# Two FFNs of a two-block transformer kernel: conditioning sums one unit later, conditioning additions in units 1 to 3 of a step

## What is computed

```python
cond = jax.nn.silu(c)
for i in range(DEPTH):                                   # DEPTH = 2
    mod = (cond @ ada_w[i] + ada_b[i]).reshape(b_, 3, 3, D_MODEL)
    h = adaln(x, norm_g[i, 0], mod[:, 0, 0], mod[:, 0, 1])
    x = x + 0.5 * (1.0 + mod[:, 0, 2][:, None, :]) * swiglu(h, ffn_w_in[i, 0], ffn_w_out[i, 0])
    ...                                                  # a mixer, then a second swiglu sublayer
def swiglu(h, w_in, w_out):                              # w_in (1024, 5632), w_out (2816, 1024)
    g, u = jnp.split(h @ w_in, 2, axis=-1)
    return (jax.nn.silu(g) * u) @ w_out
```

## Time and profile before

| what | value |
|---|---|
| median of three runs | 4431.83 us (4430.81 to 4432.5) |
| span of the profiled execution, first to last instruction | 4428.0 us |
| TensorE matmul busy | 3972.1 us, 90% |
| VectorE busy | 1926.5 us, 44% |
| ScalarE busy | 1401.3 us, 32% |
| chain of work that ended last: TensorE, VectorE, ScalarE | 78%, 9%, 6% |

### The profile page before, as it was taken

The page is one execution under the profiler, slowest core; times in us unless marked ns, Lnnn a source line. Parts: engine busy times, 40 slices in busy tenths (PEclk is TensorE's granted clock), DMA queues, the critical chain, the costliest instruction groups (busy, mean ns, idle before and its releaser), DMA issues.

```text
span 4428.0 us, 45107 instructions
## 1 busy us (share of the span) xinstructions
PE 3972.1 (90%) x16532; PEld 3063.7 (69%) x16532; DVE 1926.5 (44%) x2693; ACT 1401.3 (32%) x2072; POOL 145.5 (3%) x106
## 2 busy tenths in 40 slices
PE   6999599999999789999777789999987786998999
PEld 5887488878877347887344668778862465787887
DVE  6632775333332533333345554443335447444332
ACT  3222322232233533323333332332233333323221
POOL 1000200000000000000000000000001000000000
PEclk8999799999999689999887779999997885999999
DMA  7733376333333002333110113323330110232332
GB/s 258 240 113 88 106 254 208 93 89 95 94 89 89 0 1 79 97 95 113 29 34 5 43 38 96 91 86 96 95 97 5 34 44 5 76 99 78 99 93 88
DMA packets 626887, 390.79 MB, mean 88 GB/s; under 512 B 17088, under 2 KB 584256, under 8 KB 625600
## 3 DMA queue, kind: packets, MB, share of 16 engines
q1 hardware_dynamic: 621376, 376.82, 29.0%
q10 hardware_dynamic: 5376, 12.14, 0.8%
HBM read 386.81 MB, written 2.10 MB: 88 GB/s over the span
## 4 chain that ended last, share of the span: by engine, by line
PE 78%; DVE 9%; ACT 6%; issue 3%; DMA 2%; POOL 1%; SPq 0%; ACTq 0%; DVEq 0%; POOLq 0%
PE bank L1611 21%; PE bank L1613 21%; PE bank L1612 21%; PE bank L1770 3%; DMA work<-in_ada_w 1%; PE bank L1738 1%; ACT w_hi L638 1%; PE bank L1762 1%; PE bank L1718 1%; PE bank L1626 1%; DVE ada_acc L1039 1%; PE bank L1627 1%; PE bank L1628 1%; PE bank L1857 1%; PE bank L1637 1%
## 5 line engine op out<-in xcount | busy, mean ns | idle before, releaser
L1022 DVE TENSOR_TENSOR w_lo<-stage,w_hi 128x1024 fp32r<-128x1024 f32 x587 | 720.3, 1227 | 1825.5 <-ACT w_hi L638 1825.4
L1611 PE MATMUL bank<-h_hi,w_hi 128*128 128x512 f32 x3128 | 1229.2, 393 | 46.7 <-DVE h_lo L1274 32.3
L1613 PE MATMUL bank<-h_hi,w_lo 128*128 128x512 f32 x3128 | 1223.2, 391 | 0.0
L1612 PE MATMUL bank<-h_lo,w_hi 128*128 128x512 f32 x3128 | 1222.4, 391 | 0.0
L638 ACT ACTIVATE w_hi<-stage 128x1024 fp32r<-128x1024 f32 x587 | 622.0, 1060 | 1852.2 <-PE bank L1613 1761.8
L1611 PEld LDWEIGHTS bank<-h_hi,w_hi 128*128 128x128 f32 x3128 | 591.1, 189 | 178.0 <-DVE h_lo L1274 34.6
L1612 PEld LDWEIGHTS bank<-h_lo,w_hi 128*128 128x128 f32 x3128 | 591.3, 189 | 123.2 <-issue 1.4
L1613 PEld LDWEIGHTS bank<-h_hi,w_lo 128*128 128x128 f32 x3128 | 590.3, 189 | 124.3
L1613 PE MATMUL bank<-a_hi,w_lo 128*128 128x512 f32 x1056 | 410.8, 389 | 0.0
L1611 PE MATMUL bank<-a_hi,w_hi 128*128 128x512 f32 x1056 | 410.8, 389 | 0.0
L1612 PE MATMUL bank<-a_lo,w_hi 128*128 128x512 f32 x1056 | 410.8, 389 | 0.0
(11 more groups left out here) (243 smaller groups left out, 3664.6 us busy)
## 6 DMA issues: line engine op xcount, KB each, us to landing
stage<-in_ffn_w_in SPq DMA_DIRECT2D x176, 512.0 KB, 3.9
stage<-in_w_in SPq DMA_DIRECT2D x108, 512.0 KB, 3.9
stage<-in_w_gate_up SPq DMA_DIRECT2D x88, 512.0 KB, 3.8
ada_stage<-in_ada_w SPq DMA_DIRECT2D x128, 256.0 KB, 4.4
work<-in_ada_w SPq DMA_DIRECT2D x128, 256.0 KB, 6.0
stage<-in_ffn_w_out SPq DMA_DIRECT2D x64, 512.0 KB, 4.1
stage<-in_w_down SPq DMA_DIRECT2D x32, 512.0 KB, 3.9
stage<-in_ffn_w_out SPq DMA_DIRECT2D x32, 384.0 KB, 3.4
```

Of the source, the lines that this page charges most:

```text
L1022: nc.vector.tensor_tensor(w_lo[:, w * WORDS:(w + 1) * WORDS], stage[:, slot * WORDS:(slot + 1) * WORDS], w_hi[:, w * WORDS:(w + 1) * WORDS ...
L1611: nc.tensor.matmul(dst, wh, chunk(hi, k), start=first and a == 0, stop=False)
L1612: nc.tensor.matmul(dst, wh, chunk(lo, k), start=False, stop=False)
L1613: ins = nc.tensor.matmul(dst, wl, chunk(hi, k), start=False, stop=last and a == len(ks) - 1)
```

## The change

Two things change, in the first two FFNs alone.

1. The table of VectorE's additions goes from 6, 6, 4, 0 at the places c = 0, 1, 2, 3 of a step to 0, 6, 5, 5.
2. The sum of vector j on TensorE, which stood at the end of step j behind unit 4j + 3, stands in step j + 1 between its units 0 and 1. VectorE's `ada_finish` goes from the end of step j to place c = 1 of step j + 1, between the split and `prod`. One step more is written out for this behind the loop.

```diff
-ADA_ADDS = [0, 6, 12, 16, 16]
+ADA_ADDS = [0, 0, 6, 11, 16]
...
-                def step_in(j, ada):
+                def step_in(j, ada, finish):
                     for c in range(4):
...
                         convert(c + 2, j)
+                        if c == 1 and finish:
+                            ada_finish(j, 1)
                         if c % 2:
...
-                    if ada:
-                        ada_finish(j)
...
-                    looped(dve, count, lambda j: step_in(j, True))
-                    with dve.Fori(count, FC // 2) as j:
-                        step_in(j, False)
+                    step_in(0, True, False)
+                    with dve.Fori(1, count) as j:
+                        step_in(j, True, True)
+                    step_in(count, False, True)
+                    with dve.Fori(count + 1, FC // 2) as j:
+                        step_in(j, False, False)
...
-                def step_in(j, ada):
+                def step_in(j, add):
                     for c in range(4):
                         p = n.pair + c // 2
+                        if c == 1 and add:
+                            ada_sum(j, 1)
...
-                    if ada:
-                        ada_sum(j)
...
```

More of the change, by code:

```diff
@@ L1040, in ada_add, with ada_finish @@
                         .then_inc(ada_added, 1)
-            def ada_finish(v=0):
-                dve.wait_ge(mod_summed, n.vec - ADA_FIRST + v + 2)
-                col = (n.vec + v) * DC
+            def ada_finish(v, back):
+                dve.wait_ge(mod_summed, v + (n.vec - ADA_FIRST - back + 2))
+                col = v * DC + (n.vec - back) * DC
                 dst = mod[:, col:col + DC] if isinstance(v, int) else mod[:, bass.ds(col, DC)]
@@ L1119, in step_in @@
                                                     ALU.subtract).then_inc(a_ready, 1)
-                    if ada:
-                        ada_finish(j)
                 count = ADA_IN.get(i, 0)
                 if count:
-                    looped(dve, count, lambda j: step_in(j, True))
-                    with dve.Fori(count, FC // 2) as j:
-                        step_in(j, False)
+                    step_in(0, True, False)
[4 more added lines that the diff above has]
+                        step_in(j, False, False)
                 else:
-                    looped(dve, FC // 2, lambda j: step_in(j, False))
+                    looped(dve, FC // 2, lambda j: step_in(j, False, False))
                 n.vec += count
@@ L1630, in first_pair, with ada_sum @@
                             ins.then_inc(unit_done, 1)
-            def ada_sum(v=0):
-                pe.wait_ge(ada_added, (n.vec - ADA_FIRST + v + 1) * ADA_PER_VEC)
-                pe.wait_ge(mod_ready, n.vec + v)
+            def ada_sum(v, back):
+                pe.wait_ge(ada_added, v * ADA_PER_VEC + (n.vec - ADA_FIRST - back + 1) * ADA_PER_VEC)
+                pe.wait_ge(mod_ready, v + (n.vec - back))
                 for c in range(DC):
@@ L1667, in step_in @@
                         products((UP if c % 2 else GATE)[p % 2][:], c, range(DC), h_hi, h_lo, True, True, j)
-                    if ada:
-                        ada_sum(j)
                 count = ADA_IN.get(i, 0)
                 if count:
-                    looped(pe, count, lambda j: step_in(j, True))
-                    with pe.Fori(count, FC // 2) as j:
+                    step_in(0, False)
+                    with pe.Fori(1, count) as j:
+                        step_in(j, True)
+                    step_in(count, True)
+                    with pe.Fori(count + 1, FC // 2) as j:
                         step_in(j, False)
```

## The result

| kernel | median of its runs | ratio to before, 95% interval |
|---|---|---|
| before, same chip | 4432.16 us (4430.81 to 4434.69) | |
| changed | 4663.36 us (4659.36 to 4672.34) | 1.0518 (1.0502 to 1.0534) |

The account below looks back on a forecast made before the run. TensorE's path bounds the kernel; late weight loads make a step 35.2 us, 38.2 with slow clock, instead of 25.5. Over 16 steps that adds 203 us to the 4428.0 span, forecast 4635 us with the median's 3.8, range 4553 to 4675.

Parts of the forecast that it names:

- What bounds it, and who else waits: TensorE's path bounds the kernel; in the FFN steps ScalarE's split waits for a weight load landing 5.8 us after issue.
- The chain of twelve steps: One FFN step from VectorE's split of unit 4j + 4 to the next: 35.2 us, 38.2 with slow clock.
- step 3: Landing of the weights of unit 4j + 5 behind two loads of ada_w: 4.6 us, ends 3.5 and 5.8.
- step 7: TensorE's sum and unit 4j + 5, to the high split: 7.58 us, plus 2.99 at half clock.
- `ada_finish` and the moved sum: Moving the sum removes its 0.9 us wait and no work; ada_finish ahead of prod shows 0.08 us.
- steps 8 to 10: Splits of unit 4j + 7, 2.32 us; mod, prod, additions 0 to 3, 2.80; issue of unit 4j + 8's weights, 1.17.
- What hides elsewhere: Weights of units 4j + 6 and 4j + 7 are issued later but cost nothing, covered by the stall.
- zero: The moment when VectorE has split unit 4j + 4, where the chain of a step starts.
- Full clock: Rival: stalls, but TensorE at 2.4 GHz before the sum; 35.2 us a step, 4553 to 4600 us; chance 0.17.
- Only one late load: Rival: weights of unit 4j + 5 in time; 27.5 us a step, 4464 us, up to 4512; chance 0.06.
- The other side, faster: Rival: unit 4j + 4's weights land in time, waits go; 14 to 28 us less, 4404 to 4418; chance 0.03.
- the signs that I had named: Steps 36 to 40 us, two ScalarE load waits each, TensorE waits 7 to 8 and 3 to 4, clock about 0.8.

Follow-up runs that it names:

- the two kernels with one load in time: Changed kernel with the weight load of unit 4j + 5, or that of 4j + 4, moved ahead in SyncE's queue: 4528.08 us and 4569.79 us.
- the kernel with the sum alone: Changed kernel with the additions' table put back, so only sum and ada_finish moved against the kernel before: 4401.69 us, ratio 0.9920.
- the kernel with only unit 4j + 4 late: Changed kernel with weights of unit 4j + 5 ahead of loads m = 12 to 15 in SyncE's queue: 4528.08 us, ratio 1.0206.
- The kernel with the loads two places later: Changed kernel with SyncE's loads of ada_w two places later in its queue: 4432.88 us, ratio 0.9992 to the kernel before.

## Why the prediction was right, and where it was short

*What bounds it, and who else waits.* This was right. The load that landed 5.8 us after its issue and made ScalarE wait in the earlier trace rows was the sign; the two kernels with one load in time show that both loads count.

*The chain of twelve steps.* The turn shown above confirms its mechanism link by link. From the split of unit 4j + 4 at 199.80 to the next at 240.35, in the order of the prediction, with its numbers behind:

| step | measured | predicted |
|---|---|---|
| 1 and 2, additions 6 and 7, issue | 2.1 | 2.1 |
| 3, landing behind two loads | 5.6 | 4.6 |
| 4 and 5, splits, prod, five additions | 6.3 | 6.3 |
| 6 and 7, sum and unit, slow clock | 11.9 | 10.7 |
| 8, 9, 10, splits, additions 0 to 3, issue | 6.3 | 6.3 |
| 11, landing behind four loads | 5.95 | 5.8 |
| 12, splits | 2.4 | 2.4 |
| sum | 40.55 | 38.2 |

*The two terms that were mis-sized* are step 3 and the clock of step 7. In step 3 I took the landing nearer to the lone load (3.8 us), because only two loads stood ahead. Over the 14 turns between the sums it was 5.0 to 5.8 us, 5.3 in the mean, near the upper end. (The 3.8 of the earlier trace rows is the median of 14 loads, nine of this matrix and five of the next; the nine alone have 3.7.) And 1.2 GHz lasted long enough, in the turn shown, to cover the sum and 5.5 us of the unit; the stretch of the earlier trace rows that I took it from was shorter. Sum and unit take 11.3 us in the mean, where I had 10.6. The landing behind four loads was 4.8 to 6.6 us, 5.9 in the mean, and so as forecast.

The mean step is 39.6 and not 40.55, 1.4 us above the forecast: 0.7 for step 3 and 0.7 for the clock. By 16 that is 22 of the 28 us that the forecast was short. Of the other 6, 2 lie between the span of a profiled execution and the median of the runs (6.2 us here, and I had taken the 3.8 of before); the rest stays open. The kernel behind these steps keeps its times: from the last sum to the end it takes 3688.8 us, and the kernel with the sum alone, whose last sum stands at the same place, 3685.0. The slow sum and unit there account for the difference (11.7 against 7.5).

*`ada_finish` and the moved sum.* The moved sum costs nothing by itself, as forecast. The prediction put what there was to gain at 28 us; the sum alone gained 1.9 us a step, 30 by 16, and 0.8% in all, about 35. The 0.9 us that it gave each sum's wait is a mean over unlike waits: the first sums of the two FFNs waited 2.36 and 2.84 us, the other 14 waited 0.56 to 0.97, 0.6 in the mean. The two long ones lie outside the windows, which fits a whole gain of more than 30. That `ada_finish` ahead of `prod` costs 0.08 us is in the 6.3 of steps 8 to 10 and was not tried alone.

*What hides elsewhere.* I wrote that the weights of unit 4j + 6 are covered by the stall. ScalarE did wait for them, which is why its waits number 46 and not 32, but TensorE did not. The time that I gave for these splits was wrong: 21 us after zero and later. The one of unit 4j + 6 started at 216.66, 17 us after zero, since it waits only for the end of unit 4j + 4 and for its weights, and not for the sum. TensorE needs it only at the end of unit 4j + 5, near 225.7. That fits "covered", and no run took this cover away alone.

*The rivals.* Full clock is excluded by 0.80 in the windows. Only one late load is excluded too, and its price was too low: the kernel with only unit 4j + 4 late took 31.5 us a step, where I had 27.5, or 30.5 with the clock. The other side, faster, is what the sum does where the additions stay. Of the signs that I had named, two were off. One is the count of ScalarE's waits, as said above. The other is the waits ahead of the sum: they are 97.9 / 16 = 6.1 us, not 7 to 8, since unit 4j + 4 comes behind a gap too (3.92 us at 199.85) and starts at half the clock, so it ends later and the idle time behind it is shorter. The wait ahead of unit 4j + 4 was 61.0 / 18 = 3.4 us, as forecast.

## What to carry to other kernels

Where one in-order queue issues two kinds of load and one kind waits for compute, moving that compute moves the other kind too. Before moving the compute, follow every wait in the queue to the load behind it, and work out how much time each load has before the work that needs it. Moving a consumer later (the sum) gave slack; moving producers later (the additions) took it from loads that nobody had named. A stall of TensorE has a second price at the clock, so add it when a wait of some microseconds appears.

## What the runs showed of the hardware

*Granted clock.* In the kernel before it was 0.96 in these steps. Fourteen of the 16 sums followed a wait of 0.56 to 0.97 us and took 1.94 us. One of them, and a matmul of the unit behind it that is shown with 0.63 us, where the others at full clock have 0.39:

```profile
178.28 1.94 PE L1637 MATMUL bank<-consts,ada_acc 128*128 128x1 f32 x16 [0.56 <-DVE ada_acc L1039]
...
181.72 0.63 PE L1611 MATMUL bank<-h_hi,w_hi 128*128 128x512 f32 x1
```

This happened behind 5 of the 14, and sum and unit then took 9.2 us instead of 7.6. With the sum moved and no wait ahead of it, the clock was 1.00 in all 14 steps of both windows, although the sum stayed, and no unit behind a sum was slow. So a wait of under 1 us and the one-column matmuls behind it were enough to bring stretches of 1.2 GHz in some steps, and without the wait the full clock was back. Of the gain of 1.9 us a step, about 0.6 is the wait and most of the rest these stretches. The kernel with the loads two places later has the sum at its new place and shows the same from the other side: a wait of 1.0 us at each sum, slow stretches behind 9 of 16, and 0.96 again.

*Landing.* A weight load behind two loads of ada_w landed after 5.0 to 5.8 us, hardly sooner than one behind four (4.8 to 6.6 in the same kernel), where one alone takes 3.7 to 3.8. The single transfers of one burst tell where the time goes. In the kernel before, the four loads of ada_w issued from 190.35 on landed after 2.7, 2.7, 4.0 and 4.1 us, and the weights behind them after 5.8; in the changed kernel the two from 200.62 on landed after 2.7 and 2.8 us, and the weights, third in their burst, after 5.6 (a weight load alone takes 1.0 us more than the first load of ada_w in a burst). So in both a step of more than 1 us stands at the third transfer, whichever kind it is, and two loads ahead are enough to meet it. What makes it is open; no run here separates it.
